# A list of steps for five engines: generated by rules, or written out stage by stage

## The reference, cut to what matters

```python
h = rmsnorm(x, norm_w);  proj = h @ w_in
ya = moba_attention(aq, ak, av) * silu(ag)             # 8 heads
yb = head_norm(retention(rot(bq), rot(bk), bv)) * silu(bg)
yc = head_norm(mlstm(conv(cq), conv(ck), cv, ci, cf) * sigmoid(co)) * silu(cg)
x = x + concat(ya, yb, yc) @ w_out                     # after two layers: rmsnorm
```

## Time and profile before

| | |
|---|---|
| median of 3 runs | 2367.08 us (2366.47 to 2372.52) |
| profiled execution, span | 2371.1 us |
| PE busy | 2288.5 us, 97% of the span |
| PE weight loads busy | 1953.8 us, 82% |
| DVE busy | 1589.4 us, 67% |
| ACT busy | 887.5 us, 37% |
| POOL busy | 243.7 us, 10% |
| granted TensorE clock, mean | 0.986 |

### The profile page before, as it was taken

How to read it: one execution, slowest core, us unless ns; L and a number is a source line. 1 busy time by engine, 2 the same in 40 slices (tenths; PEclk the granted TensorE clock), 3 DMA queues, 4 the chain that set the end, 5 groups by cost and what they waited for, 6 DMA issues and landing times.

```text
span 2371.1 us, 33029 instructions
## 1 busy us (share of the span) xinstructions
PE 2288.5 (97%) x13198; PEld 1953.8 (82%) x13198; DVE 1589.4 (67%) x2898; ACT 887.5 (37%) x1507; POOL 243.7 (10%) x321
## 2 busy tenths in 40 slices
PE   7988989999999999999999999999999999998998
PEld 6878879988888777777888888888888887898998
DVE  5887886888877457774599866654333456876665
ACT  5444444422223344433322222332222235554443
POOL 1101102000102100022111111200000120021001
PEclk9998999999999999999999999999999999998999
DMA  7534534655653312223256665323222232354553
GB/s 264 179 124 162 186 116 152 229 202 174 221 173 126 102 60 65 67 88 103 90 208 230 210 212 196 132 87 109 89 98 93 95 116 96 105 171 141 184 186 116
DMA packets 97657, 341.31 MB, mean 144 GB/s; under 512 B 11312, under 2 KB 13488, under 8 KB 97120
## 3 DMA queue, kind: packets, MB, share of 16 engines
q1 hardware_dynamic: 74144, 254.46, 32.0%
q0 software_dynamic: 23360, 84.74, 11.1%
HBM read 338.11 MB, written 2.48 MB: 144 GB/s over the span
## 4 chain that ended last, share of the span: by engine, by line
PE 79%; DVE 12%; issue 4%; ACT 4%; POOL 1%; DMA 0%; POOLq 0%; DVEq 0%; ACTq 0%
PE PS L595 77%; DVE WL L1269 3%; ACT WH L965 1%; PE PS L916 1%; DVE HL L1278 1%; DVE NT L1278 1%; POOL ACC L1867 1%; ACT P L966 1%; DVE PJB L1278 1%; DVE CV L1278 1%; DVE JK L1279 1%; DVE AR L1279 1%; ACT HH L965 0%; DVE P L1273 0%; DVE ST L1282 0%
## 5 line engine op out<-in xcount | busy, mean ns | idle before, releaser
L965 ACT ACTIVATE WH<-RAW 128x1024 fp32r<-128x1024 f32 (+3 forms) x498 | 511.5, 1029 | 974.2 <-PE PS L595 974.2
L595 PE MATMUL PS<-HH,WH 128*128 128x512 f32 (+1 forms) x2240 | 776.2, 347 | 11.8 <-DVE HL L1278 5.7
L595 PE MATMUL PS<-HH,WL 128*128 128x512 f32 (+1 forms) x2240 | 767.4, 343 | 0.0
L595 PE MATMUL PS<-HL,WH 128*128 128x512 f32 (+1 forms) x2240 | 767.3, 343 | 0.0
L1269 DVE TENSOR_TENSOR WL<-RAW,WH 128x1024 fp32r<-128x1024 f32 (+3 forms) x498 | 589.0, 1184 | 122.4 <-ACT WH L965 121.3
L595 PEld LDWEIGHTS PS<-HH,WH 128*128 128x128 f32 x2240 | 425.7, 190 | 75.1 <-DVE HL L1278 9.5
L595 PEld LDWEIGHTS PS<-HH,WL 128*128 128x128 f32 x2240 | 425.6, 190 | 52.3
L595 PEld LDWEIGHTS PS<-HL,WH 128*128 128x128 f32 x2240 | 425.8, 190 | 51.1
L595 PE MATMUL PS<-GH,WH 128*128 128x512 f32 (+1 forms) x776 | 271.0, 349 | 0.0
L595 PE MATMUL PS<-GH,WL 128*128 128x512 f32 (+1 forms) x776 | 270.7, 349 | 0.0
L595 PE MATMUL PS<-GL,WH 128*128 128x512 f32 (+1 forms) x776 | 270.5, 349 | 0.0
(11 more groups left out here) (220 smaller groups left out, 2798.6 us busy)
## 6 DMA issues: line engine op xcount, KB each, us to landing
RAW<-in_wst SPq DMA_DIRECT2D x436, 512.0 KB, 3.5
AR<-in_w_adaT POOLq DMA_DIRECT2D x144, 512.0 KB, 3.8
RAW<-in_wst SPq DMA_DIRECT2D x48, 384.0 KB, 3.0
BM<-rpb_rows POOLq DMA_DIRECT2D x48, 64.0 KB, 3.0
CB<-in_cc POOLq DMA_DIRECT2D x2, 1024.0 KB, 11.2
RAW<-in_wst SPq DMA_DIRECT2D x8, 256.0 KB, 2.7
RAW<-in_wst SPq DMA_DIRECT2D x4, 396.0 KB, 3.2
rpb_rows<-in_rpb POOLq DMA_DIRECT2D x2, 697.5 KB, 12.2
```

What stands on the lines that cost most here:

```text
L595: return e.matmul(o, l, r, start=start, stop=stop)
L965: return e.activation(o, i, f, bias=bias, scale=scale)
```

## The change

The list is no longer made by rules. It is written out as text, `ORDER`, one string for each of nine stages, and `spell` turns it into letters (`3*ND` is NDNDND). `mix`, `BORDER`, `normalise_first`, `until` and the loop that put in H, S and V are gone. Units, steps, tiles, banks, buffers, every instruction and every wait are the same, and so is the number of each letter (1044 D, 498 H, 498 S, 522 V, 150 N, 146 E, 132 B, and so on). Within a letter the order is the same too. What differs is how the letters interleave: of the letters that PE has, 422 of 1476 places hold another letter than before; on ACT 908 of 1598, on DVE 1001 of 1663, on POOL 327 of 947. The nine stages hold D0 to 85, 86 to 179, 180 to 235, 236 to 345, 346 to 481, 482 to 629, 630 to 777, 778 to 907 and 908 to 1043: the first model's layers, its end with the second model's start, the first SwiGLU block, mixer 1, two SwiGLU blocks, mixer 2, and the last SwiGLU block. The diff, cut to its core (lines of `ORDER` that the text speaks of):

```diff
-def mix(**steps):
...
-        out += [((2 * i + 1) / (2 * n), name) for i in range(n)]
-    return [name for _, name in sorted(out, key=lambda x: x[0])]
+ORDER = (
+
+    "NNHSHHDNNN 3*ND DDDNDNDHDSVVHSSDMSMHSDVV DHSVSHDHSSHVVDVDHMHDTDVD VSSDHDMDSDHMTDSDMHMHSDMM "
...
+    "ESMTDSDTMDHSHAHDVMHDVDDD VMSDMMSEHDSMHASVDDVASDHD AMSVHDVDASVMADDDDHVHSMAV SDDDHDAVADHSDDSDVAVADHDD "
...
+    "DDNNDNNNNNVESDHDV HMSDDSHDVDVDHEDVSHMHVDDS QDHSVMDHHDDQSADVSDMDVSDH VDMHEVSVMTDHDSDSHMDDVVME "
...
+    "DHSDBVDBPVBDHBBHHSVVDDBD SVSBBDPBPDDSDHBDBSHVVHBH PBVDCDSHDCVDCSBBBSCHBBDC SVVBHBDDSDDBCHHVDBDDCBBB "
...
+def spell(text):
+
+    names = []
+    for word in text.split():
+        n, _, group = word.rpartition("*")
+        names += list(group) * int(n or 1)
+    return names
...
-        order += mix(D=8, M=7, E=1)
...
-    BORDER = ["("]
-    BORDER += ["D", "V", "N", "D", "N", "V"]
...
-    order += ffn(0, 0, "1", 512, nw, 0, HELD) + B + BORDER
-    order += mixer(0, False, 4) + B + BORDER
...
-    def until(name, k):
-        out.extend([name] * max(0, k - n[name]))
-        n[name] = max(n[name], k)
...
-            if name == "D" and not by_hand:
-                e = n["D"] // 2
-                if n["D"] % 2:
-                    until("H", due[e + 1])
-                    until("V", e)
-                else:
...
-                    until("S", due[e])
-                    until("V", e - lag)
-    order = normalise_first(out + ["V"] * (len(S) - n["V"]))
+    order = [name for stage in ORDER for name in spell(stage)]
```

More of the change, by code:

```diff
@@ L55, in plan @@
+def spell(text):
[4 more added lines that the diff above has]
+    return names
 def plan():
-    U, S, T, order = [], [], [], []
+    U, S, T = [], [], []
     in_bank, ropes, att = {}, {}, {}
@@ L130, in silu @@
[L130 to L145, removed]
+            att[l, i - 2] = T[tile("att", l, i - 2, 256)]
@@ L146, in plan @@
+        for i in range(4):
+            feat("w_in", l, 1536 + 128 * i, 1, "silu", "H1", l, 256, 8 + i)
+        heads(2)
+        for i in range(2):
+            feat("w_in", l, 4096 + 128 * i, 1, "silu", "H1", l, 256, 18 + i)
+        heads(3)
         if l == 0:
-            def out1(i):
+            for i in range(0, 8, 2):
                 pairs("w_out", l, 4, 4, "o1", "Y1", l, 4, 256, i, 1)
[L150 to L157, removed]
+                if i == 2:
+                    heads(4)
+            heads(5)
             pairs("w_out", l, 0, 4, "o0", "Y1", l, 0, 256)
-            order += mix(D=4) + ["^"]
     def ctx(n):
         passes([first.pop(0) for _ in range(n)], BOTH[:1])
-    pairs("w_out", 1, 4, 4, "o1", "Y1", 1, 4, 256, 0, 1)
-    order += ["D", "N", "D", "N"]
-    pairs("w_out", 1, 4, 4, "o1", "Y1", 1, 4, 256, 2, 1)
@@ L169, in plan @@
[L169 to L173, removed]
+    for i in range(0, 8, 2):
+        pairs("w_out", 1, 4, 4, "o1", "Y1", 1, 4, 256, i, 1)
+        if i == 4:
+            heads(4)
     first = hidden(0, 0, "1", 0, 2)
     ctx(2)
-    order += ["D", "D"] + heads(5) + ["A", "D", "D"]
+    heads(5)
@@ L196, in plan, with ffn @@
[L196 to L203, removed]
+    def ffn(f, l, name, n):
         halves = BOTH if n == 512 else None
@@ L219, in ffn @@
                 passes(us[8 - held:], halves)
[L220 to L223, removed]
     def mixer(l, last, norm):
-        out = []
         nq = 256 if last else 512
@@ L246, in mixer @@
         tokm(w, l, ((768, 1152), (1664, 1792)), (2, 2, 2, 2), "v2", "H", norm, 4, (0, 1, 2, 3))
-        out += mix(D=3 if last else 2) + ["K"] + mix(D=2) + ["F", "B"]
         for i in (1, 2) if last else (1, 5, 2):
@@ L257, in mixer @@
         gates(0, 0, 1, 2, 3)
[L258 to L265, removed]
         for b in range(3):
@@ L276, in mixer @@
                 gates(b + 1, 2, 3)
[L277 to L280, removed]
         if last:
             feat("w_out_2", l, 0, 8, "wo", "M", l, nq)
-            return out + mix(D=8)
+            return
         feat("w_out_2", l, 0, 8 - HELD, "wo", "M", l, nq)
@@ L286, in mixer @@
         passes(us, BOTH)
-        return out + mix(D=8 - HELD)
-    nw = 72 + 1 - 25
-    B = ["D", "D"] * HELD
-    order += ffn(0, 0, "1", 512, nw, 0, HELD) + B + BORDER
-    order += mixer(0, False, 4) + B + BORDER
[L293 to L322, removed]
+    ffn(0, 0, "1", 512)
+    mixer(0, False, 4)
+    ffn(2, 0, "2", 512)
+    ffn(3, 1, "1", 512)
+    mixer(1, True, 7)
+    ffn(5, 1, "2", 256)
     closed = {}
@@ L330, in plan @@
             S[e + 1].split.append(u + NS)
[L331 to L335, removed]
-    def until(name, k):
-        out.extend([name] * max(0, k - n[name]))
-        n[name] = max(n[name], k)
[L341 to L351, removed]
-        else:
[L353 to L359, removed]
-            if name == "D" and not by_hand:
-                e = n["D"] // 2
-                if n["D"] % 2:
-                    until("H", due[e + 1])
-                    until("V", e)
-                else:
-                    if ahead or n["D"] == soon:
-                        until("V", e)
-                    until("S", due[e])
-                    until("V", e - lag)
-    order = normalise_first(out + ["V"] * (len(S) - n["V"]))
+    order = [name for stage in ORDER for name in spell(stage)]
     return U, S, T, order, ropes, att
```

58 lines of the change are left out of this document (36 added, 22 removed).

## The result

The kernel after takes 2308.27 us (median of 4 runs, 2307.91 to 2308.74), beside 2368.73 us for the kernel before on the same chip (4 runs, 2366.47 to 2372.52). The ratio is 0.974, with a 95% interval of 0.9727 to 0.9752: 60.5 us less. The forecast was 2342, with a range down to 2314.

What follows compares the result with a forecast made beforehand. PE was taken to bound the kernel, idle for 82.6 of 2371.1 us. Gains of 6.0, 10.0, 2.5, 3.0, 0.5, 1.0 and 6.0 less 4.0 us made 25.0, for a median of 2342 us; range 2314 to 2363, the forecast's own 2322 to 2355.

Steps and rivals of the forecast that it cites:

- What bounds the kernel: Whole kernel: PE sets the end, idle for 82.6 of 2371.1 us; the change can only move idle time and what depends on it.
- mLSTM's ends: Last mLSTM step in both layers of the first model: two equal PE waits, 6.9 us together, shrink; 6.0 us gained.
- splits: All stages: PE's 14.1 us of waits for splits shrink as casts and splits stand further ahead; 10.0 us gained.
- second model's attention: Attention jobs of the second model, longest wait in mixer 2: 2.5 of 3.3 us gained.
- norms: Norm chains through ACT, POOL, PE and DVE: 3.0 of 20.2 us of waits gained, since the chain itself stays.
- retention: Retention's output, two waits at A0 and A12: 0.5 of 3.8 us gained, producer and consumer spaced as before.
- start: Square sums at the kernel's start: N0 goes ahead of S0 and S1; bounds 0 and 2.4, 1.0 us gained.
- the clock: Three half-clock stretches right behind PE waits, 15.0 us of PE work: bounds 0 and 7.5, 6.0 us gained.
- new waits: Unevenly spaced attention jobs, as in mixer 1, may wait for their data: bounds 0 or 48 us, 4.0 us lost.
- It goes further: Rival: nearly all 49.5 us of waits and 7.5 us of clock go, median 2310 us; chance 0.13.
- The waits only move on: Rival, first two layers: removed waits return at the next split, leaving 2358.5 us, or 2362 with new waits; chance 0.13.
- Hoisted chain steps hold up splits: Rival, first model's layers: earlier chain steps delay splits on DVE, 6.3 us per place, ten places give 2401 us; chance 0.10.

Runs made afterwards that it cites:

- e8: The kernel after with PE made to wait at 15 steps of one SwiGLU block for the eviction of the step just before: 2351.72 us, ratio 0.9918.
- e3: The kernel before with four halves of a step instead of two behind M31 and M64, in both mLSTM layers, nothing else: 2368.49 us, ratio 0.9985.
- e5: The kernel before with M6 to M30, M39 to M63 and all of T three halves of a step further ahead: 2372.26 us, ratio 1.001.
- e11: The kernel after with four letters moved at its four longest split and eviction waits: 2311.02 us, beside 2309.86 for the unchanged list on the same chip.
- e18: The kernel before with M33 moved ahead of H48 and E8 ahead of V47, to free split 50: 2367.07 us, ratio 0.999.
- e1: The written list for the first three stages (up to D235), the rules' list of the kernel before from there on: 2327.17 us, ratio 0.9807.
- e2: The rules' list of the kernel before up to D235, the written list for the other six stages: 2350.87 us, ratio 0.9911.
- e13 to e17: Five kernels: the kernel before with some kinds of letters at written places in the first three stages: 2365.96, 2405.6, 2442.94, 2448.33 and 2404.67 us.

## Why the prediction was wrong, point by point

**What bounds the kernel** was read rightly: PE sets the end, and the gain lies where PE was idle. That DVE in the first layers "has only a fifth to a quarter of DVE's time to win" was no limit: in layer 2 the written list leaves DVE 8% idle and PE 1%.

**The terms of the sum**, from the profiled executions (25.0 us forecast, 65.1 measured):

| term | taken | measured | from |
|---|---|---|---|
| mLSTM's ends | 6.0 | 6.9 | no TM wait left |
| splits | 10.0 | 6.6 | WL 14.1 to 7.5 |
| second model's attention | 2.5 | 3.3 | no P wait left |
| norms | 3.0 | 7.0 | DG, HL, SQ 20.2 to 13.2 |
| retention | 0.5 | 3.8 | no RT wait left |
| start | 1.0 | 1.4 | SS 11.2 to 9.8; 0.2 of it at the start, 1.2 at a norm in stage 3 |
| the clock | 6.0 | about 16 | 52.7 to 16.9 us of PE's work at 0.50 |
| new waits | -4.0 | -3.7 | MG 1.6 more, five new kinds 2.1 |
| waits outside rows 3, and gaps | none | 12.8 | 12.0 and 0.8 |
| inside busy time | none | about 11 | the rest |

The direction was right; two steps of the sum failed. The first is the clock: "bounds 0 and 7.5". That was the price of the three stretches of rows 9, taken for the whole; the trace had eleven, with 52.7 us of PE's work in them instead of 15.0. Halved as the prediction halves it, that is a bound of 26.4 us. Eight of the eleven are gone after, and the term is some 10 us of the miss. That waits in full work do make such stretches is shown by e8. Halving is a little too much: the spacing of matmuls gives 0.44 of the time back, not 0.5.

The second is the 49.5 us taken for all the idle time that could go. Rows 3 hold 59.5 of the 82.6 us of idle time; the 23.1 us in smaller waits and gaps were in no term and no bound. They gave 12.8 us. The new waits were sized well (3.7 us, taken 4.0), but by luck: they were to come from the uneven distances between attention jobs, and no wait for P is left at all.

A third part, about 11 us inside what the records call busy, had no term either. Its cause stays open; some 4 us of it may be that the profiled execution of before was a long one.

The other terms missed by a few microseconds each. Norms and retention were taken "nearest to nothing since the chain itself stays": the chains' work stays, but 7.0 and 3.8 us of their waits went. Splits gave less than taken (6.6 of 10.0): in mixer 2 PE's waits for them grew from 1.1 to 3.5 us.

**The reasoning behind the terms** was also weaker than two right sizes suggest. The prediction followed a wait, found the letters that stand in front of it, and priced its removal with the clock behind it. Done alone at two places this gave 3.5 and 2.7 us where 11 and 6.3 were expected. At mLSTM's ends the wait mostly moved on (TM 2.9 us less, HC 2.5 more). At split 50 it went as read, and only the clock's part of the price failed. Nor is the gain a sum of such places: the list is one arrangement of chains, casts, splits and evictions, which gives 44.8 us in three stages as a whole and a loss in most of its parts.

**The rivals.** "It goes further" came, though not as worded: 38.1 us of idle time went and not 49.5, and the clock gave about 16 and not 7.5; that the time comes within 2 us of its 2310 is luck. "The waits only move on" is false of the change, true of several edits (e3, e5, e11), and false of one (e18). "Hoisted chain steps hold up splits" is false of the written list, and true when the chains go ahead alone (WL 21.3 us, e5). Its price of 6.3 us for a wait of 2.9 us was too high: e18 won 2.7 us with one, and by e8 it costs 4.1 to 4.6 on average.

Shown by runs: the gain is local to the stages (e1, e2); no kind of letters carries it alone (e13 to e17, first three stages); waits of up to 4.1 us in full work bring stretches at half clock, but not each of them does (e8, e2). Open: which of the relations between letters matter most, chains and evictions together, and what the 11 us within busy time are.

## What to carry to other kernels

Price the clock by all of its low stretches, counted from end to end, and bound the idle time by the whole of it, not by the rows that are shown. Before small waits of two traces are compared, look at a second execution of the same program: a fall of the clock hides the waits behind it, and here it came in one execution and not in the other. In a kernel whose engines all follow one order, a local edit can remove one wait or move it along (the four here gave between nothing and 3.5 us), and a small result from one says nothing about what a whole new order can give. An order that takes over part of a good one can be worse than either whole (here by 35 to 78 us than the list before).

## What the runs showed of the hardware

Waits forced at fifteen places, of at most 4.1 us each in otherwise full work, brought six stretches at the 1.2 GHz level, of 3.4 or 6.8 us each (e8). Whether a given wait draws one can differ between executions: behind the wait of 2.9 us at D100 the clock stood at 0.50 for 6.8 us in the trace of before and stayed at 1.00 in that of e2, with the same letters up to there. At 0.50 the starts of matmuls lay 1.8 times as far apart as at 1.00, not twice (0.214 us against 0.119 on 256 columns, 0.427 against 0.232 on 512).
